# Twelve whole float32 weight pages of block two turned into pages in high and low halves

## The reference, cut to what matters

```python
xn = rmsnorm(h, norm1_g[layer])
proj = xn @ w_in[layer]
q_a, k_a, v_a, q_r, f_r, i_r, g_r = jnp.split(proj, IN_SPLITS, axis=-1)   # 7 pieces of 512 columns
attn = moba_attention(q_a..., k_a..., v_a...)      # 8 heads of 64
rec = hgrn2(q_r, f_r, i_r, g_r, lb, norm_g)        # 4 heads of 128, a gated recurrence
h = h + jnp.concatenate([attn, rec], axis=-1) @ w_out[layer]
h = h + peer(rmsnorm(h, norm2_g[layer]), ...)      # each token gathers 128 expert rows and sums them
```

## Time and profile before

| what | us |
|---|---|
| median of 3 runs (1426.35 to 1428.86) | 1427.47 |
| the profiled execution's own time | 1430.86 |
| its span in the trace | 1429.1 |
| PE busy, share of the span | 1298.3, 91% |
| DVE busy | 827.0, 58% |
| ACT busy | 609.9, 43% |
| POOL busy | 545.7, 38% |
| chain that ended last: PE, DMA | 61%, 26% of the span |

### The profile page before, as it was taken

The page is one execution under the profiler, slowest core; times in us unless marked ns, Lnnn a source line. Parts: engine busy times, 40 slices in busy tenths (PEclk is TensorE's granted clock), DMA queues, the critical chain, the costliest instruction groups (busy, mean ns, idle before and its releaser), DMA issues.

```text
span 1429.1 us, 22155 instructions
## 1 busy us (share of the span) xinstructions
PE 1298.3 (91%) x8588; PEld 911.0 (64%) x8588; DVE 827.0 (58%) x1884; ACT 609.9 (43%) x1432; POOL 545.7 (38%) x374
## 2 busy tenths in 40 slices
PE   7999999999999999999998999999777777787786
PEld 6888897788999999997897544444222222222222
DVE  3865200355457873477324866677766666677754
ACT  3210221256566665553453544444434444444433
POOL 1100000004878888740042544434444344433441
PEclk9999999999999999999998999999999999999999
DMA  6332321334545556543367999999999999999995
GB/s 238 118 111 90 103 87 59 101 105 148 176 162 186 186 184 196 168 133 94 137 242 307 369 422 421 421 421 422 421 421 421 422 422 421 422 410 422 419 421 235
DMA packets 67652, 381.05 MB, mean 267 GB/s; under 512 B 7520, under 2 KB 7648, under 8 KB 34528
## 3 DMA queue, kind: packets, MB, share of 16 engines
q0 software_dynamic: 36864, 268.45, 45.4%
q1 hardware_dynamic: 29808, 107.49, 22.7%
q10 hardware_dynamic: 880, 3.76, 0.8%
HBM read 378.63 MB, written 1.05 MB: 266 GB/s over the span
## 4 chain that ended last, share of the span: by engine, by line
PE 61%; DMA 26%; ACT 6%; DVE 3%; POOL 2%; issue 2%; DVEq 0%; POOLq 0%; ACTq 0%
PE bank L420 25%; DMA arena_block<-in_experts,arena_block 25%; PE bank L1006 9%; PE bank L454 4%; PE bank L965 4%; PE bank L472 3%; PE bank L418 2%; PE bank L436 1%; PE bank L835 1%; POOL arena_block L2231 1%; PE bank L505 1%; ACT arena_block L1476 1%; ACT L1464 1%; ACT L1470 1%; ACT arena_block L1474 1%
## 5 line engine op out<-in xcount | busy, mean ns | idle before, releaser
L1006 PE MATMUL bank<-arena_block 128*128 128x512 f32 x1024 | 493.4, 615 | 107.8 <-ACT arena_block L1476 107.6
L1006 PEld LDWEIGHTS bank<-arena_block 128*128 128x128 f32 x1024 | 181.0, 191 | 408.3 <-ACT arena_block L1476 256.6
L2159 DVE SCALAR_TENSOR_TENSOR ring<-arena_block 128x1024 f32<-128x1024 f32 x256 | 313.2, 1225 | 196.9 <-DMA arena_block<-in_experts,arena_block 160.3
L2215 POOL TENSOR_TENSOR w_lo<-ring,w_hi 128x1024 fp32r<-128x1024 f32 x108 | 261.7, 2443 | 432.6 <-ACT w_hi L1065 432.2
L2231 POOL DMA_INDIRECT arena_block<-in_experts,arena_block x256 | 273.2, 1067 | 388.7 <-PE bank L1006 348.7
L1470 ACT ACTIVATE arena_block<-arena_block 128x1 f32<-128x1 f32 x256 | 51.8, 202 | 324.8 <-DVE ring L2159 323.4
L1065 ACT ACTIVATE w_hi<-ring 128x1024 fp32r<-128x1024 f32 x108 | 113.6, 1054 | 59.4 <-PE bank L454 28.8
L420 PE MATMUL bank<-h_norm,ring 128*128 128x256 f32 x480 | 112.9, 390 | 0.0
L420 PE MATMUL bank<-x_hi,w_hi 128*128 128x256 f32 x384 | 109.2, 284 | 1.6 <-POOL w_lo L2215 1.5
L420 PE MATMUL bank<-arena_mix,ring 128*128 128x256 f32 x480 | 109.9, 385 | 0.1
L420 PE MATMUL bank<-x_lo,w_hi 128*128 128x256 f32 x384 | 108.7, 283 | 0.0
(11 more groups left out here) (486 smaller groups left out, 2030.4 us busy)
## 6 DMA issues: line engine op xcount, KB each, us to landing
ring<-in_pages SPq DMA_DIRECT2D x189, 512.0 KB, 3.6
late<-in_pages SPq DMA_DIRECT2D x11, 512.0 KB, 6.1
arena_block<-in_experts,arena_block POOLq DMA_INDIRECT x256
x_res<-in_xT SPq DMA_DIRECT2D x2, 512.0 KB, 5.0
arena_mix<-in_memT ACTq DMA_DIRECT2D x1, 1024.0 KB, 10.5
arena_block<-in_subkT ACTq DMA_DIRECT2D x1, 1024.0 KB, 5.0
out_tok<-arena_block SPq DMA_DIRECT2D x4, 256.0 KB
const<-in_const ACTq DMA_DIRECT2D x1, 974.5 KB, 7.4
```

What stands on the lines that cost most here:

```text
L1006: last = mm(bank[2 * tt + j][:, :], diag[:, slot, :], uv[slot][:, D + j * 512:D + (j + 1) * 512], start=False, stop=stop)
L2159: stt(junk[r % 2], uv[s][:, 0:D], 1.0, htok[:, tt, :], ALU.mult, ALU.mult, accum_out=e_act[:, s:s + 1])\
L2215: nc.gpsimd.tensor_tensor(w_lo[:, slot, :], ring[:, slot, :], w_hi[:, slot, :].bitcast(F32), ALU.subtract)\
```

## The change

One list is shortened: the pages of `qk` and `ti` are no longer in `WHOLE`, those of `g2` still are. Everything else follows from the lists `SPLIT` and `NTH`.

```diff
-WHOLE = list(range(PAGE0["qk"], PAGE0["out2"])) + list(range(PAGE0["wq"], N_PAGES))
+WHOLE = list(range(PAGE0["g2"], PAGE0["out2"])) + list(range(PAGE0["wq"], N_PAGES))
```

## The result

The changed kernel takes 1438.96 us (median of 5, 1435.32 to 1441.80), the kernel before 1427.47. The ratio is 1.0077, with a 95% interval of 1.0066 to 1.0088: **slower by 11 us**. The forecast was 1433.1, in a range of 1425 to 1439. The direction is right, but the time lies 0.04 us inside the upper end of the range. That it lies inside at all is luck, and the size has to be explained.

The account below looks back on a forecast made before the run. PE was taken as the bound, at full clock. Shorter pages -9.24, late page 0 +0.69, DVE and POOL turns +12.63 and clock +1.5 gave +5.6 us: median 1433.1, range 1425 to 1439.

Parts of the forecast that it names:

- What bounds the kernel, and where the shift goes: PE at full clock bounds the stage the change touches; a shift there moves the end by the same amount.
- Part 1: PE's twelve pages in `qk` and `ti` take 2.88 us each in place of 3.65: -9.24 us.
- Part 2: New ACT copies and POOL subtractions are in ample supply; only page 0 comes late: +0.69 us.
- Part 3: In the units, POOL subtractions and DVE's SBUF instructions run one after the other, whole; PE waits: +12.63 us.
- The 0.95 at `mb_flip(0)`: PE's added wait there, in us, because the fifth POOL subtraction holds L1990 for 1.6 us.
- The sixth and ninth: POOL subtractions of the twelve; the sixth was to hold L1996 for 2.15 us, the ninth L1957 for 2.3.
- the tenth: POOL subtraction not among those forecast to add waits; the others were to fall where DVE waits for PE anyway.
- the eleventh and twelfth: POOL subtractions forecast to hold L1943 for 2.1 us and head 5's L1996 for 2.15; together +3.04 us of PE waits.
- Part 4: PE's clock drops to half behind long waits, at least once: +1.5 us taken, from 0 to 5.
- The sum: Over the whole kernel: +4.1 us from pages and waits, +5.6 with the clock, so the median becomes 1433.1.
- the clock again and again: Rival with chance 0.07: PE's clock drops repeatedly, making the kernel slower.

Follow-up runs that it names:

- e2: The changed kernel with GpSimd's subtraction for the twelve pages cut to 16 of 1024 columns, so their low halves are left out; ratio 0.9966 to the kernel before, 1424.32 us.
- e1: The kernel before plus only the twelve pages' ScalarE copies and GpSimd subtractions, halves unused, TensorE still multiplying whole pages; ratio 1.0042, 1435.56 us.
- e8: The changed kernel with each of the twelve subtractions cut into two pieces of 128x512; ratio 1.0040 to the kernel before, 1435.77 us.
- e3: The changed kernel with each of the twelve subtractions cut into eight pieces of 128x128, the same work; ratio 1.0048 to the kernel before, 1435.78 us.
- e7: The changed kernel once more, unedited, on the chip of other follow-up runs; ratio 1.0058 to the kernel before.

## Why the prediction was right, and where its size was off

- **What bounds the kernel, and where the shift goes: right.** Behind the stage the two profiles agree within 0.2 us. That they agree so closely is partly luck, since in the profiles of the other kernels this part took 724 to 732 us.
- **Part 1, pages: right in kind, 2.28 us too much.** The products do come every 0.12 us, but a page takes 3.07 and not 2.88, so the term is -6.96 and not -9.24; e2 measured -6.8. The row I took is of the `down` stage, where page follows page. In the units a page follows other matmuls: its first product takes 0.22 in place of 0.12, and the next other matmul begins 0.21 after its last one. The Trainium skill, *FP8 and Floating Point Precision*, section TensorE Precision Notes, would make it three quarters of 3.65; the trace has 3.07, 84%, and the measurement decides.
- **Part 2, page 0 late by 0.69: right.** 0.58 and 0.55 in the two profiles of the change.
- **Part 3, turns of DVE and POOL: mechanism right, 2.96 us too much.** e1 and e2 show it from both sides. Waits grew by 10.36 (page 0's included) where 13.32 were forecast. `mb_score(0)` waited 3.43 (forecast 4.07) and `h_pairs(3)` 0.93 (0.94). The 0.95 at `mb_flip(0)` did not come: L1990 was held for 0.58 us, not 1.6, since it began late in the fifth subtraction. The sixth and ninth met L1957 and L1996, the two forecast in the other order, and the tenth met L1956, which was forecast free; the eleventh and twelfth held L1943 and L1996 as forecast.
- The Trainium skill, *SBUF — State Buffer*, section Who interferes with whom, says that the port is locked for a whole instruction. e8 agrees with it: instructions of half the length hold DVE half as long, 1.1 us in place of 2.2. e3 shows more than a hold of one instruction: 6.97 us, through 15 of them.
- **Part 4, the clock: the step that failed.** I took 1.5 us, for one slow stretch, and 5 as the most. There were five, 7.5 us in all (three and 4.8 in e7, the changed kernel's other profile). The reason for one was a single row, in which PE was busy for 1.21 of 3.41 us, and I let only the longest wait count fully. In fact the clock also fell at the waits of 0.93 and 1.31 that lie 2 us apart, in both profiles, and behind those of 2.47 and of 1.44, in the first one only. A slower PE then shifted the stage, but didn't shorten the waits.
- **The sum.** -6.96 + 10.36 + 7.54 = +10.94, which is the difference of the two profiled runs, 1441.80 - 1430.86; the medians differ by 11.49. Pages and waits were both too large in size and nearly made up for each other (+3.4 in place of +4.1), which is luck. So the miss in the profiled runs, +10.9 for +5.6, is the clock's: 6.0 us too little for it, 0.7 too much for the rest. In e7 the stage is +7.38, and the clock's part of the miss is 3.3. What the prediction calls *the clock again and again*, with a chance of 0.07, is what happened. It should have had a large share of the forecast's 0.74, because every long wait that part 3 counted could bring a drop, though not each one did.

## What to carry to other kernels

Before work is given to an idle GpSimd, look at what VectorE does in the same microseconds: each meeting with a VectorE TENSOR_TENSOR on two SBUF operands, or with a TENSOR_SCALAR or COPY within SBUF, costs up to the whole length of the GpSimd instruction, however short VectorE's own is. A TENSOR_REDUCE from SBUF and whatever reads a bank ran on undisturbed here. When a forecast adds waits to an engine that was always busy, give every long wait its chance of a slow stretch, not the longest alone; here the clock cost 7.5 us beside 10.4 us of added waits, and 4.8 beside 9.5 in e7. And take the length of a block of matmuls from a place with the same neighbours.

## What the runs showed of the hardware that was not expected

- Subtractions of 128x1024 (2.40 us) or 128x512 alternate with a waiting DVE instruction (e7, e8). A gap-free row of 128x128 ones did not: it held one DVE instruction for 6.97 us (e3).
- A TENSOR_REDUCE of 128x256 from SBUF took 408 ns inside a subtraction, as elsewhere.
- A subtraction of 128x128 starts every 0.42 us in a row, so eight of them take 3.4 us where one of 128x1024 takes 2.40.
- The granted clock went to 0.50 for about 3.4 us behind stretches in which PE was busy for 1.96 of 3.40 us, and also went on at 0.50 behind one at half clock in which it was busy for 2.97 of 3.41. But in e7 it stayed at 1.00 behind one in which PE was busy for 1.00 of 3.41. By the accounts of the stages one slow stretch cost 1.5 to 1.8 us, and 0.9 in e3, where a wait of 6.51 us reached into them.
- The first product of a page behind other matmuls takes 0.22 us, the next ones 0.12; at half clock they are 0.21 apart.
